# A third seven-product block in 11 of 15 feed-forward groups, with the convolution's border products on ScalarE

## What is computed

```python
def conv_glu_ffn(h, w_gate, w_up, conv_w, conv_b, w_down):
    g = h @ w_gate
    u = h @ w_up
    gp = jnp.pad(g, ((0, 0), (CONV_WIDTH - 1, 0), (0, 0)))
    g = conv_b + gp[:, 0:S] * conv_w[0]
    for j in range(1, CONV_WIDTH):          # CONV_WIDTH = 3
        g = g + gp[:, j:j + S] * conv_w[j]
    return (jax.nn.gelu(g, approximate=True) * u) @ w_down
```

## Time and profile before

| what | value |
|---|---|
| median of 3 runs | 1419.64 us (1419.17 to 1419.71) |
| the profiled execution | 1419.19 us, span 1417.4 us |
| PE busy | 1406.1 us, 99% of the span, 6502 matmuls |
| DVE busy | 1235.0 us, 87% |
| ACT busy | 822.2 us, 58% |
| POOL busy | 358.5 us, 25% |
| mean granted clock of TensorE | 0.999 |

### The profile page before, as it was taken

One profiled execution on the slowest core, in us unless ns is written; L12 is line 12 of the kernel. 1 busy time (PEld: TensorE's weight loads), 2 busy tenths in 40 slices (PEclk: granted clock), 3 DMA queues, 4 the chain that ended last, 5 costly groups with the idle time before them and its releaser, 6 DMA issues.

```text
span 1417.4 us, 18897 instructions
## 1 busy us (share of the span) xinstructions
PE 1406.1 (99%) x6502; PEld 1172.3 (83%) x6502; DVE 1235.0 (87%) x1867; ACT 822.2 (58%) x1082; POOL 358.5 (25%) x609
## 2 busy tenths in 40 slices
PE   9999999999999999999999999999999999999997
PEld 9888888888878888888888888888888888888886
DVE  6867778975587899989999999999998999999996
ACT  7455544554475656655655655556656666666663
POOL 0702020620003234443324444234444000000000
PEclk9999999999999999999999999999999999999999
DMA  8765656555557677767677776677777576666662
GB/s 265 223 182 158 193 183 192 164 164 178 178 165 242 198 228 238 237 208 228 213 219 240 234 228 208 219 227 224 231 231 240 177 236 212 209 198 210 202 214 93
DMA packets 149706, 293.75 MB, mean 207 GB/s; under 512 B 17232, under 2 KB 30832, under 8 KB 149360
## 3 DMA queue, kind: packets, MB, share of 16 engines
q1 hardware_dynamic: 132416, 274.71, 61.6%
q0 software_dynamic: 16384, 16.81, 4.3%
q10 hardware_dynamic: 816, 1.09, 0.2%
HBM read 273.67 MB, written 2.10 MB: 195 GB/s over the span
## 4 chain that ended last, share of the span: by engine, by line
PE 93%; DVE 4%; DMA 1%; ACT 1%; issue 0%; SPq 0%; POOL 0%; DVEq 0%; ACTq 0%
PE psum L2115 48%; PE psum L1888 7%; PE psum L1892 7%; PE psum L1890 7%; PE psum L2096 5%; PE psum L2098 5%; PE psum L2097 5%; PE psum L1855 3%; DVE w_lo L1595 2%; PE psum L1859 2%; DMA stage<-in_w_qkv 1%; PE psum L1936 0%; DVE up_T L1606 0%; PE psum L1942 0%; ACT w_hi L927 0%
## 5 line engine op out<-in xcount | busy, mean ns | idle before, releaser
L2115 PE MATMUL psum<-w_hi,hT 128*128 128x512 f32 x1696 | 463.4, 389 | 0.0
L2115 PEld LDWEIGHTS psum<-w_hi,hT 128*128 128x128 f32 x1696 | 318.3, 188 | 66.2 <-issue 0.2
L2115 PE MATMUL psum<-w_lo,hT 128*128 128x512 f32 x848 | 261.1, 389 | 0.0
L1125 DVE TENSOR_TENSOR w_lo<-stage,w_hi 128x1024 fp32r<-128x1024 f32 x141 | 175.5, 1250 | 90.0 <-ACT w_hi L657 88.6
L657 ACT CAST w_hi<-stage 128x1024 fp32r<-128x1024 f32 x141 | 147.8, 1051 | 179.3 <-PE psum L1892 142.5
L1595 DVE TENSOR_TENSOR w_lo<-stage,w_hi 128x1024 fp32r<-128x1024 f32 (+1 forms) x198 | 219.4, 1136 | 11.4 <-ACT w_hi L927 11.4
L1097 POOL DMA_DIRECT2D gate_rows_f<-gate_T x256 | 134.8, 536 | 368.4 <-DVE gate_T L1472 315.6
L927 ACT CAST w_hi<-stage 128x1024 fp32r<-128x1024 f32 (+1 forms) x198 | 190.1, 984 | 57.0 <-PE psum L2115 42.0
L2115 PEld LDWEIGHTS psum<-w_lo,hT 128*128 128x128 f32 x848 | 159.2, 188 | 33.0
L1097 POOL DMA_DIRECT2D up_rows_f<-up_T x256 | 134.6, 534 | 45.4 <-DVE up_T L1472 36.0
L1888 PE MATMUL psum<-w_hi,hT 128*128 128x512 f32 x312 | 124.9, 400 | 0.0
(11 more groups left out here) (256 smaller groups left out, 2584.4 us busy)
## 6 DMA issues: line engine op xcount, KB each, us to landing
stage<-in_w_qkv SPq DMA_DIRECT2D x93, 512.0 KB, 3.7
stage<-in_w_gate SPq DMA_DIRECT2D x88, 512.0 KB, 4.2
stage<-in_w_up SPq DMA_DIRECT2D x88, 512.0 KB, 5.2
stage<-in_w_down SPq DMA_DIRECT2D x84, 512.0 KB, 4.7
stage_wide<-in_w_down SPq DMA_DIRECT2D x42, 512.0 KB, 4.5
stage_early<-in_w_gate SPq DMA_DIRECT2D x40, 512.0 KB, 4.2
stage_early<-in_w_up SPq DMA_DIRECT2D x40, 512.0 KB, 5.2
stage<-in_w_o SPq DMA_DIRECT2D x32, 512.0 KB, 3.9
```

Source lines behind the costliest of these rows:

```text
L1125: nc.vector.tensor_tensor(w_lo[s][:, :], stage[s][:, :], w_hi[s][:, :].bitcast(F32), ALU.subtract).then_inc(s_lo, 1)
L2115: ins = nc.tensor.matmul(c_bank(G, t, c), a[:, j, ROWS[t]], w[slot_of[v]][:, COLS[c]], start=(q == 0 and j == 0 and n == 0), stop=False, s ...
```

## The change

- In the first 11 groups (`THREE_IN`) block 5 is summed too. Its sums of activations are kept in `h_sums_early`, which lies where the gated rows of later groups are written.
- In a summed block of a group the low parts of the two raw units stand between the three weight sums instead of behind them. SP's queue also waits for the sums before it loads over a summed block's stage.
- The products over the seven borders are made on ScalarE (`edge_products`, eight Copy activations with a scale column into a spare tile, at n = 10) and added on VectorE by two additions over all four channel tiles (`add_edges`). Taps 1 and 0 on VectorE keep only their large operations.
- Steps: gate and up bank sums (`add_rows`) go from n = 1, 2 to n = 2, 3; `conv_tap_2` from 10 to 9, which lies in summed block 4, so ScalarE runs gating steps in summed blocks too; `conv_tap_1` and `conv_tap_0` are at 12 and 13 in the first 11 groups and at 11 and 12 after them. `joint_products` stays behind block 7.
- GpSimd's moves are written as one loop; their order is the same.

```diff
-F_SUMMED = (2, 4)
+F_SUMMED = (2, 4, 5)
+EARLY_GROUPS, ALWAYS = 11, 2
+THREE_IN = tuple(range(EARLY_GROUPS))
...
+        edge_1 = diag[:, 0, 0:(BLOCKS - 1) * CT].rearrange("p (q f c) -> p q f c", q=BLOCKS - 1, f=CT)
+        edge_0 = diag[:, 1, 0:(BLOCKS - 1) * CT * 2].rearrange("p (q f c) -> p q f c", q=BLOCKS - 1, f=CT)
...
-        SUMS_AT = tuple(10 + 2 * x for x in range(len(F_SUMMED)))
-        GATE_ADD_AT, UP_ADD_AT, ACT_SCALE_AT, GATE_TURN_AT, UP_TURN_AT = 1, 2, 3, 3, 7
-        CONV_AT, GATED_AT, ACT_GELU_AT = (10, 11, 13), 15, 15
+        SUMS_AT = tuple(9 + 2 * x for x in range(len(F_SUMMED)))
+        GATE_ADD_AT, UP_ADD_AT, ACT_SCALE_AT, GATE_TURN_AT, UP_TURN_AT = 2, 3, 3, 3, 7
+        CONV_AT, CONV_AT_THREE, GATED_AT, ACT_GELU_AT, ACT_EDGE_AT = (9, 11, 12), (9, 12, 13), 15, 15, 10
...
-        SUMS = (F_SUMMED,) * F_GROUPS + SUMMED
+        SUMS = tuple(F_SUMMED if G in THREE_IN else F_SUMMED[:ALWAYS] for G in range(F_GROUPS)) + SUMMED
...
                     sp.wait_ge(s_lo, unit_taken(stage_before[u]))
+                    if is_ffn_summed(stage_before[u] // 2):
+                        sp.wait_ge(s_w_sum, 3 * sums_before(stage_before[u] // 2) + 3)
...
+            def edge_products(i):
+
+                wait_from(act, s_edge, 2 * i)
+                for w, e, n in ((1, edge_1, 1), (0, edge_0, 2)):
+                    for j in range(CT):
+                        f = i * CT + j
+                        nc.scalar.activation(e[:, :, j, :], gate_F[:, 0:BLOCKS - 1, j, QUADRANT - n:QUADRANT], ACT.Copy,
+                                             scale=conv_c[:, w, f:f + 1]).then_inc(s_edge_product, 1)
...
+                if n == ACT_EDGE_AT:
+                    edge_products(i)
...
                     if g >= D0:
                         gated_sum_high(g)
+                    else:
+                        gating_steps(G, 2 * q)
                     sum_high(g, 0)
                     sum_high(g, 1)
+                    if g < D0:
+                        gating_steps(G, 2 * q + 1)
...
                     add_tap(1, j, i, act_F[:, :, j, 1:QUADRANT], gate_F[:, :, j, 0:QUADRANT - 1], s_conv_1)
-                    add_tap(1, j, i, act_F[:, 1:BLOCKS, j, 0:1], gate_F[:, 0:BLOCKS - 1, j, QUADRANT - 1:QUADRANT],
-                            s_conv_1)
...
+            def add_edges(i):
+
+                dve.wait_ge(s_edge_product, (i + 1) * (2 * CT))
+                for n, e in enumerate((edge_1, edge_0)):
+                    dve.wait_ge((s_conv, s_edge)[n], ((i + 1) * CT, 2 * i + 1)[n])
+                    dst = act_F[:, 1:BLOCKS, :, 0:n + 1]
+                    nc.vector.tensor_tensor(dst, dst, e, ALU.add).then_inc(s_edge, 1)
...
                 weight_sum_13(g)
+                unit_low(g, 0, CHUNK)
                 weight_sum_2(g)
+                unit_low(g, 1)
                 weight_sum_4(g)
```

More of the change, by code:

```diff
@@ L139, in layer_kernel @@
         post_g = sb("post_g", [P, D])
-        h_sums = nc.alloc_sbuf_tensor_at("h_sums", [P, len(F_SUMMED), 2, 2, SEQ], F32R, offset=post_at)
+        h_sums = nc.alloc_sbuf_tensor_at("h_sums", [P, ALWAYS, 2, 2, SEQ], F32R, offset=post_at)
         ffn_g_at = (nc.sbuf_base + 31) // 32 * 32
@@ L216, in layer_kernel, with h_sums_of @@
             w_lo.append(place(f"w_lo{s}", [P, UNIT], F32R))
+        h_sums_early = place("h_sums_early", [P, 1, 2, 2, SEQ], F32R, at=44 * KIB)
+        def h_sums_of(x):
+            return h_sums[:, x, :, :, :] if x < ALWAYS else h_sums_early[:, x - ALWAYS, :, :, :]
         for s in range(len(EARLY_SLOTS)):
@@ L356, in layer_kernel @@
         QUADRANT_MOVES = (P // QUADRANT) ** 2
-        s_conv = sem("conv_ready")
+        s_conv = sem("conv_taps_added")
+        s_edge_product = sem("conv_block_edge_products")
+        s_edge = sem("conv_block_edges_added")
         s_gelu = sem("gelu_ready")
@@ L431, in layer_kernel @@
                   + [(F_GROUPS + p, q) for p in range(PASSES) for q in range(PAIRS)])
-        SUMS = (F_SUMMED,) * F_GROUPS + SUMMED
+        SUMS = tuple(F_SUMMED if G in THREE_IN else F_SUMMED[:ALWAYS] for G in range(F_GROUPS)) + SUMMED
+        JOINT_AT = tuple(blocks.index((G, CHUNK_UNITS - 1)) if G < F_GROUPS
+                         else blocks.index((G, 0)) + SUMS[G][-1] + 3 for G in range(len(SUMS)))
         FIRSTS = [blocks.index((G, 0)) for G in range(len(SUMS))]
@@ L503, in quarters, with is_ffn_summed @@
             return pair_stage(g).rearrange("p (b n) -> p b n", b=4)
+        def is_ffn_summed(g):
+            return 0 <= g < D0 and is_summed(g)
         def w_sum_of(g):
@@ L523, in p_bank, with conv_at @@
             return bank[4 * (G % 2) + n]
+        def conv_at(i):
+            return CONV_AT_THREE if i in THREE_IN else CONV_AT
         x_rows = x.rearrange("(t p) d -> p t d", p=P)
@@ L866, in normed_sum_high @@
                 act.wait_ge(s_h_sum, 4 * (x + 1))
-                nc.scalar.copy(h_sums[:, x, 0, :, :], h_sum).then_inc(s_h_sum_hi, 1)
+                nc.scalar.copy(h_sums_of(x)[:, 0, :, :], h_sum).then_inc(s_h_sum_hi, 1)
             def conv_tap_2(i):
@@ L951, in take_first_product @@
                 if G < F_GROUPS:
-                    act.wait_ge(s_conv, (G + 1) * (2 * CT))
+                    act.wait_ge(s_edge, 2 * (G + 1))
                 nc.scalar.copy(y_of(G, 0, 0), p_bank(G, 0)[:, :]).then_inc(s_p1, 1)
@@ L962, in gating_steps @@
                         scale_rows(i, 1)
-                if n == CONV_AT[0]:
+                if n == conv_at(i)[0]:
                     conv_tap_2(i)
+                if n == ACT_EDGE_AT:
+                    edge_products(i)
                 if n == ACT_GELU_AT:
@@ L982, in _ @@
                             gating_steps(G, 2 * q + j)
-                if g - 3 in ENDS:
-                    take_first_product(ENDS.index(g - 3))
+                if g in JOINT_AT:
+                    take_first_product(JOINT_AT.index(g))
                 if g == D0 + PAIRS + 3:
@@ L1105, in move_up @@
                 move_quadrants(i, turned[1], up_F, s_up_turned, s_up_F)
-            move_gate(0)
-            for i in range(1, F_ITERS):
-                move_up(i - 1)
+            for i in range(F_ITERS):
                 move_gate(i)
-            move_up(F_ITERS - 1)
+                move_up(i)
             inverse_root_of(0, 6)
@@ L1511, in gated_rows @@
                 dve.wait_ge(s_gelu, i + 1)
-                if i >= min(RETIRED_AT):
+                if i >= EARLY_GROUPS:
                     dve.wait_ge(s_used, block_used(LASTS[i - 1]))
@@ L1540, in normed_sum_low @@
                 dve.wait_ge(s_h_sum_hi, x + 1)
-                nc.vector.tensor_tensor(h_sums[:, x, 1, :, :], h_sum, h_sums[:, x, 0, :, :].bitcast(F32),
+                nc.vector.tensor_tensor(h_sums_of(x)[:, 1, :, :], h_sum, h_sums_of(x)[:, 0, :, :].bitcast(F32),
                                         ALU.subtract).then_inc(s_h_sum_lo, 1)
@@ L1643, in sums, with sums_and_unit_lows @@
                 nc.vector.tensor_tensor(s4, a12, s2, ALU.subtract).then_inc(s_a_sum, 1)
-            def sums_of_weights(g):
+            def sums_and_unit_lows(g):
                 before = [h for h in range(g) if is_summed(h)]
@@ L1691, in gating_steps @@
                     turn_up(i)
-                if n == CONV_AT[1]:
+                if n == conv_at(i)[1]:
                     conv_tap_1(i)
-                if n == CONV_AT[2]:
+                if n == conv_at(i)[2]:
                     conv_tap_0(i)
+                    add_edges(i)
                 if n == GATED_AT:
@@ L1713, in _ @@
                         gated_sum_low(g)
+                        unit_low(g, 1)
                     else:
-                        sums_of_weights(g)
-                        unit_low(g, 0, CHUNK)
-                    unit_low(g, 1)
+                        sums_and_unit_lows(g)
                     for n in range(2):
@@ L1726, in _ @@
                             gating_steps(G, 2 * q + j)
-                if g - 3 in ENDS:
-                    joint_products(ENDS.index(g - 3))
+                if g in JOINT_AT:
+                    joint_products(JOINT_AT.index(g))
                 if g == D0 + PAIRS + 2:
@@ L2090, in summed_rows_of @@
                 q = blocks[g][1]
-                return h_sums[:, F_SUMMED.index(q), part, :, :] if g < D0 else (a_hi, a_lo)[part](entry[g] + 1)
+                return h_sums_of(F_SUMMED.index(q))[:, part, :, :] if g < D0 else (a_hi, a_lo)[part](entry[g] + 1)
             def rows_product(o, rows, g, w, cs, j, ts, start):
```

6 lines of the change are left out of this document (2 added, 4 removed).

## The result

The changed kernel takes **1441.82 us** (median of 4 runs, 1440.05 to 1442.86) against 1419.48 us before: a ratio of 1.0156, 95% interval [1.0139, 1.0174]. It is 22.3 us slower; 15.7 had been worked out.

A forecast was written before the change was run, and what follows sets the result against it. TensorE bounds the kernel before; VectorE was to become the bound in three-sum groups. -7.48 + 22.1 + 1.4 - 0.3 = +15.7 us on 1419.19 gives 1434.9, on the median's level 1435.4, said as 1435; range 1420 to 1444.

The forecast's parts named there:

- The cycle had been put at 43.8: Three-sum group: 43.0 us of VectorE work plus 0.8 lost to ScalarE, 2.3 more than TensorE's.
- the 43.0 of the list: VectorE's operations in a three-sum group, added up to 43.0 us against TensorE's 41.48, trusted to 0.3 us.
- the sum: Whole kernel: -7.48 products, +22.1 waits in groups 1 to 10, +1.4 group 11, -0.3 ending, giving +15.7 us.
- the scaled Copy: Scaling of 512 columns on ScalarE, nearest relative of one edge product, from which 0.20 us each was taken.
- the prediction's clock: Times in a three-sum group counted from 0, the start of block 4's last weight sum on VectorE.
- The lead of 0.9 us: VectorE's spare time before block 5's last slot, taken off 23.0 us to leave 22.1 of TensorE waits, groups 1 to 10.
- 28.3 against 29.2: Microseconds after the group's start when VectorE at best, and TensorE, reach block 5's last slot.
- That is enough without a queue's delay: Gate moves: 8.4 us issue plus some 4 us landing fit the about 15 us between transpose and tap product.
- put at +1.4: First group after the three-sum groups, entered without lead, costs about 1.4 us.
- the taps come a unit earlier: Last gating group: Gelu waits for its own high part alone, gated product some 0.7 us sooner; counted -0.3.
- ScalarE hides its edges: Rival: VectorE bounds but the 0.8 us ScalarE loss becomes 0; +6.7, about 1426 us; chance 0.15.
- TensorE stays the bound: Rival: VectorE's list 1.5 us too long; -7.5, 1412 us; sign turns at a 42.35 us cycle; chance 0.08.

The follow-up runs named there:

- late_edges: The changed kernel with the border products at step 12 instead of 10 in the eleven three-sum groups, behind block 5's high parts on ScalarE: 1437.04 us.
- two_blocks: The changed kernel without its third summed block (THREE_IN empty), everything else of the change kept, tap 2 still at step 9: 1423.29 us.
- eleven_old_steps: The changed kernel with border products at step 12 everywhere and the taps of groups 11 to 15 back at steps 10, 11, 13: 1432.02 us.

## Why the prediction was right or wrong

**The mechanism was right**: VectorE becomes the bound from group 1 to 10, at a cycle above the old 42.16. The cycle had been put at 43.8; measured are 43.68 and 44.03 in turn. That it is so near is in part luck: without any wait for ScalarE (late_edges) the cycle is 43.22 or 43.57, 0.2 to 0.6 us above the 43.0 of the list, and the wait was 0.45 where 0.8 had been put. The list of VectorE's work held as busy time: 42.9, and two removals and one addition of work (tap 0, the wait in block 5, the borders) moved the even groups by 1.74, 0.46 and 0.57 us where the operations themselves said 1.70, 0.45 and 0.55. Of the 6.6 us that the sum lacked, groups 1 to 10 hold 3.1, group 0 0.1, what lies behind group 11 3.9; group 11 and the opening take 0.3 each off.

**The border products** step 0.20 us (8 in 1.69), the value taken from the scaled Copy. VectorE's wait behind them was 0.45 where 0.8 had been put. On the prediction's clock (0 is 724.07 in group 6) the high part was ready at 7.74 us, as worked out, but VectorE wanted it at 7.33 and not at 7.03, because single steps at the end of block 4 and the start of block 5 are 0.07 to 0.12 us longer than their fellows. The Trainium skill ("ScalarE: Activation LUTs", section "Rules for kernel authors") has 0.3 us per ACTIVATE: the duration of one is 0.296 us here, and neighbours overlap by a third of it. Priced by that rule the case would have been 1444; the trace decides for 0.20, and the 1441.8 us measured came about by other terms (below).

**The two additions** were put at 0.46 and took 0.57 us with the waits around them (from the last tap 0 at 695.04, plus 0.38, to 695.99). Small.

**The lead of 0.9 us was not there.** This step failed: it took VectorE to stand at the bank sums the moment group 1 begins. In fact TensorE can't begin a group before the joint sums of the group before, and VectorE has three more low parts between these and the bank sums, which start 2.04 us behind the group's first product (485.06 against 483.02 in group 1; 703.96 in group 6):

```profile
706.00 1.28 DVE L1716 TENSOR_TENSOR gate_rows_f<-psum,gate_rows_f 128x512 f32<-128x512 f32 x2
```

With 2.04 added, the prediction's own 28.3 against 29.2 is a deficit of 1.1 us. Group 0 ends 0.14 us over its 41.48, and group 1 already lasts 44.03, as the other odd ones do. The best case of one group was set against a sequence of groups. Five deficits of 2.20 and five of 2.55 are 23.8 and not 22.1.

**Group 4** lasts 45.17 us, 1.5 more than the other even ones, which makes 25.2 us over groups 1 to 10. GpSimd started the gate's moves 3 us after the transpose:

```profile
624.64 8.41 POOL L1136 DMA_DIRECT2D gate_rows_f<-gate_T  x16 [28.46 <-issue]
...
638.03 2.08 ACT L899 ACTIVATE act_g<-gate_rows_f,conv_c 128x256 f32<-128x256 f32 x4 [1.39 <-DMA gate_rows_f<-gate_T]
```

The same delay is in the trace of before, where tap 2 stood a unit later with slack around it. The prediction read that row and wrote "That is enough without a queue's delay"; the row had such a delay in it. 3.0 + 8.4 + 4.2 = 15.6 us from the transpose to the last landing is more than its 15. That the delay is what group 4 pays for is supported by groups 4 and 11 of two_blocks, but no run takes the delay away.

**Group 11** was put at +1.4, for entering without lead, and measured +1.1. That is luck for the most part: it is entered without lead in eleven_old_steps too and costs 0.1 there, and two_blocks, which has lead, pays 0.5. What costs is the order on ScalarE in a group where GpSimd is late.

**Behind group 11** the sum had -0.3, and measured are +3.6. The step that failed is "the taps come a unit earlier", from which "the gated product can follow some 0.7 us sooner" was concluded: only the Gelu's place in the order was looked at, not tap 2's data. The gate rows of the last group are due at the same distance from their transpose as everywhere, but the eight blocks there are plain, VectorE and ScalarE run through them to the limit of the slots, and step 9 comes before the data. The last gating blocks and the rest of the down projection lost 2.4 us by that. The 1.2 us of group 14 is the same kind: of the six slots of split weights in turn, one leaves at group 12 and one at group 14, the high parts wait for TensorE, and with tap 2 and the borders ahead of them block 5's come too late. Four slots, not six, are in turn in group 14; that this is the reason is argued from the table of slots, since no run changed it alone. That the steps are, is shown: with tap 2 at step 10, tap 0 at 13 and the borders at 12 both losses are gone.

The rivals: "ScalarE hides its edges" is what late_edges makes true, and it gives 1437, not 1426, since groups 1 to 10 still lose 20.1 us in it, where the rival had 13.5, and the losses behind them stay. "TensorE stays the bound" would have needed a cycle of 42.35; the list was within 0.2 us of the measured busy time.

In all, from 1418.6 with neither: the third block in 11 groups costs 13.5 us, the steps the other 9.8 (4.8 for the border products in the three-sum groups, late_edges against after; 5.0 for the steps of tap 2, tap 0 and the borders in the other groups, from there to eleven_old_steps).

## What to carry to other kernels

When an edit trades the bound engine's work for another's, make the second engine's list for one cycle and compare it with the new, shorter cycle of the first. Here 2.5 us of idle time a group had to pay for the 4.1 us of a third block less 0.7 us taken off elsewhere, and could not. If the list is a little too long, spend it only as often as the lead is restored: with the same steps, the third block lost 13.5 us in 11 neighbouring groups and won 2.5 us in every other one (1418.56 without it, 1432.02 and 1416.03). A step that waits for data in order, moved a unit earlier, has to be looked up at the place where the engines run furthest ahead, not in the typical cycle.
